# One mixer and MLP block kernel on a single core: the small pieces beside the big products are placed two at a time

## The reference

```python
proj = einsum('bsd,de->bse', rms_norm(x, norm_w), w_in)      # 6160 columns
# 4 GLA heads (dk 128, dv 256), 4 HGRN heads (dk 128, dv 128), each the recurrence
#   S_t = diag(g_t) S_{t-1} + k_t v_t^T,  o_t = S_t^T q_t
# 4 cross heads: softmax(q mk^T / sqrt(128)) mv over the memory's 256 tokens
mixed = concatenate([gla_o, hgrn_o, xo]) * silu(gate)        # each head rms-normed
x = x + mixed @ w_out
```

## Time and profile before

| | |
|---|---|
| median of 3 runs | 2051.71 us |
| time of the profiled execution | 2051.9 us |
| its span | 2050.1 us |
| PE busy | 2011.2 us, 98% of the span |
| PEld busy | 1687.5 us, 82% |
| DVE busy | 1070.6 us, 52% |
| ACT busy | 815.6 us, 40% |
| POOL busy | 762.3 us, 37% |
| chain that ended last | PE 81%, POOL 6%, DVE 6%, issue 3%, ACT 3% |

### The profile page before, as it was taken

How to read it: one execution, slowest core, us unless ns; L and a number is a source line. 1 busy time by engine, 2 the same in 40 slices (tenths; PEclk the granted TensorE clock), 3 DMA queues, 4 the chain that set the end, 5 groups by cost and what they waited for, 6 DMA issues and landing times.

```text
span 2050.1 us, 26312 instructions
## 1 busy us (share of the span) xinstructions
PE 2011.2 (98%) x10210; PEld 1687.5 (82%) x10210; DVE 1070.6 (52%) x1903; ACT 815.6 (40%) x1365; POOL 762.3 (37%) x441
## 2 busy tenths in 40 slices
PE   9999999999999999999999989999999999999997
PEld 7888988988988888888888867788888888888886
DVE  6264455446555365554589978897541211112125
ACT  5424232343434523132365575763544333222311
POOL 3421211111121334353359948695444443222220
PEclk9999999999999999999999999999999999999998
DMA  4311111011111586775355423232223232111112
GB/s 175 101 34 52 42 32 52 32 59 35 42 52 61 185 318 239 260 262 162 116 185 185 178 90 103 83 94 93 93 91 103 93 98 88 43 50 51 52 42 82
DMA packets 69564, 215.63 MB, mean 105 GB/s; under 512 B 7856, under 2 KB 8240, under 8 KB 69312
## 3 DMA queue, kind: packets, MB, share of 16 engines
q1 hardware_dynamic: 55472, 188.26, 27.4%
q10 hardware_dynamic: 13968, 25.70, 3.6%
HBM read 184.56 MB, written 29.36 MB: 104 GB/s over the span
## 4 chain that ended last, share of the span: by engine, by line
PE 81%; POOL 6%; DVE 6%; issue 3%; ACT 3%; DMA 0%; POOLq 0%; DVEq 0%; SPq 0%; ACTq 0%
PE B L1491 37%; PE B L1670 24%; PE B L1554 7%; POOL CO L2786 5%; PE B L1592 4%; DVE B L2214 1%; PE B L1619 1%; PE B L1616 1%; PE B L1622 1%; POOL WL L2742 1%; DVE HB L2214 1%; PE B L1655 1%; PE B L1639 1%; PE B L1579 1%; PE B L1539 1%
## 5 line engine op out<-in xcount | busy, mean ns | idle before, releaser
L1491 PE MATMUL B<-HB,WH 128*128 128x512 f32 x2976 | 933.2, 401 | 7.2 <-DVE UP L2214 3.6
L2742 POOL TENSOR_TENSOR WL<-RAW,WH 128x1024 fp32r<-128x1024 f32 x205 | 495.1, 2419 | 933.1 <-ACT WH L1886 932.0
L1491 PEld LDWEIGHTS B<-HB,WH 128*128 128x128 f32 x2976 | 549.0, 189 | 127.0 <-issue 17.6
L1491 PE MATMUL B<-HB,WL 128*128 128x512 f32 x1488 | 563.9, 392 | 1.4 <-POOL WL L2742 1.4
L1886 ACT ACTIVATE WH<-RAW 128x1024 fp32r<-128x1024 f32 x205 | 215.6, 1056 | 444.8 <-DMA RAW<-wall 425.9
L1491 PEld LDWEIGHTS B<-HB,WL 128*128 128x128 f32 x1488 | 280.7, 189 | 62.9 <-POOL WL L2742 2.9
L2214 DVE SCALAR_TENSOR_TENSOR RES<-B,modv,RES 128x512 f32<-128x512 f32 x144 | 105.3, 749 | 203.5 <-PE B L1670 176.5
L2214 DVE SCALAR_TENSOR_TENSOR B<-UP,vec,B 128x512 f32<-128x512 f32 x308 | 208.1, 751 | 0.0
L1670 PE MATMUL B<-HIDH,WH 128*128 128x512 f32 x512 | 185.5, 395 | 0.0
L1670 PE MATMUL B<-HIDH,WL 128*128 128x512 f32 x512 | 182.4, 389 | 0.0
L1670 PE MATMUL B<-HIDL,WH 128*128 128x512 f32 x512 | 182.4, 389 | 0.0
(11 more groups left out here) (246 smaller groups left out, 2532.2 us busy)
## 6 DMA issues: line engine op xcount, KB each, us to landing
RAW<-wall SPq DMA_DIRECT2D x204, 512.0 KB, 3.6
MODRAW<-wmod ACTq DMA_DIRECT2D x96, 256.0 KB, 5.0
WH<-parts SPq DMA_DIRECT2D x32, 512.0 KB, 3.3
WL<-parts SPq DMA_DIRECT2D x32, 512.0 KB, 4.2
RES<-xT SPq DMA_DIRECT2D x16, 512.0 KB, 7.6
oscr<-OT SPq DMA_DIRECT2D x32, 256.0 KB, 2.1
OI<-oscr SPq DMA_DIRECT2D x16, 512.0 KB, 5.3
parts<-WH SPq DMA_DIRECT2D x16, 512.0 KB, 5.3
```

The source lines that it names most:

```text
L1491: i = pe.matmul(bank, a[:, ks], hb(part, k, h), start=k == 0 and n == 0, stop=k == 7 and n == 2)
L2742: po.tensor_tensor(lo, raw, hi.bitcast(F32), ALU.subtract).then_inc(sig[f"w_lo{q % NW}"], 1)
```

## The change

`tick` gets a threshold `group[0]`. It is 2.0 from the first recurrent head to the last product of the mixers, and 1.0 elsewhere, where `tick` works as before. With 2.0 nothing is placed until one of the two lanes has a credit of 2.0. Then there are two rounds, and in each the recurrent lane places a step if its credit is at least 0.3, and so does the cross lane. Rates and costs of the steps are the same, and so are all instructions; only their order changes. Up to the gates' products 336 small pieces stood in 270 unbroken runs between big matmuls; now they stand in 156, of which 92 have two pieces, 29 one, 23 three, 7 four, 4 five and 1 six.

```diff
 PASS = 0.2133
+GROUP = 2.0
 ...
-    credit, rate, turn = [0.0, 0.0], [0.5, 0.0], [0]
+    credit, rate, turn, group = [0.0, 0.0], [0.5, 0.0], [0], [1.0]

     def tick(us):
         while due and now["pe"] >= due[0][0]:
             next_due()
         u_splits(at_unit[0] - 1)
         credit[0] += rate[0] * us
-        while credit[0] >= 1.0 and (bg or bg2):
-            credit[0] -= step()
+        credit[1] = credit[1] + rate[1] * us if bg3 else 0.0
+        if max(credit) >= group[0]:
+            least = 1.0 if group[0] == 1.0 else 0.3
+            for _ in range(2 if group[0] > 1.0 else 100):
+                if credit[0] >= least and (bg or bg2):
+                    credit[0] -= step()
+                if credit[1] >= least and bg3:
+                    credit[1] -= step_in(bg3)
         if not (bg or bg2):
             credit[0] = min(credit[0], 1.0)
-        credit[1] = credit[1] + rate[1] * us if bg3 else 0.0
-        while credit[1] >= 1.0 and bg3:
-            credit[1] -= step_in(bg3)
 ...
     rate[0] = RATE[0]
+    group[0] = GROUP
     for h in range(4):
 ...
     rate[0] = RATE[3]
+    group[0] = 1.0
     for h in range(2):
         gate_product(0, h)
```

## The result

The changed kernel takes 2066.29 us (median of 4 runs, 2064.80 to 2067.83) against 2050.49 us (4 runs, 2046.66 to 2052.34): ratio 1.0078 [1.0061, 1.0096], so slower by 0.8%. The forecast was 2067 us, slower. The median of before is 2050.49 and not 2051.71 because a fourth run was added. The profiled execution of the changed kernel took 2067.63 us, with a span of 2065.8; that of before had 2051.9 and 2050.1. So 15.7 us are to be explained.

A forecast was written before the change was run, and what follows sets the result against it. TensorE's own instruction list was taken as the bound. GLA pairs 4.0, HGRN 6.6, less 2.0, ScalarE 1.6, longer runs 6.8, less 1.9 gave 15.1 us on 2051.9: 2067 us, 0.7% slower, range 2059 to 2074.

The forecast's parts named there:

- Entries cost nothing with 128 columns: At runs of small pieces in the mixers: halving the entries (270 runs to 156) gives 0, at most 1 us.
- 64 columns: At the 64-column level: a crossing costs 0.32 us, one of two goes in six of eight heads, 1.9 us gained.
- Pairs of chunks, regular price: In adjacent chunks, the second waits for banks 6 and 7: GLA loses 4.0 us, HGRN 6.6 us.
- ScalarE busy ahead: 1.6 us: At chunk pairs: a ScalarE operation of 0.3 to 1 us ahead in a third of 26 pairs adds 1.6 us.
- Longer runs: 6.8 us: In longer runs of small pieces, a fourth use of three `S` banks waits for the first: nine places, 6.8 us together.
- Pairs of levels without cross steps: 0: At two adjacent level halves without cross steps: they are independent, in different banks, and cost nothing.
- Existing stops: TensorE's stops in the mixers before the change, within 8.9 us idle; the sum has no term for their going.
- rival 2: In the mixers, the new order misses existing stops, 6 us of idle goes, pair waits under 2 us: 2046 us; chance 0.07.
- Rival 3, the clock: In the mixers, stops bring the clock down, seven more such stretches, 12 us on top: 2079 us; chance 0.18.
- What would show it: From 100 to 700 us TensorE's idle rises from 8.9 to some 20 us, with `OSB`, `ST`, `AB` wait rows; afterwards only later.
- the three HGRN pairs of before: HGRN chunk pairs already adjacent before the change; their waits were taken off the sum at 2.0 us.

## Why the prediction was right

The time (2066.3 against 2067) and the sign were right, and so was the kind of cause: TensorE waits for drained banks. Its idle time in the mixers is 19.6 us against the 20 forecast. Much of the closeness is luck: the mixers got 13.5 us longer, not 15.1, and the start's -1.4 and the end's +3.6 of the clock are no part of the argument. By its steps:

- **Entries cost nothing with 128 columns.** Right. Of the 201 single pieces before, the six with the largest excess hold 6.1 us, all at waits; the other 195 have 0.65 us together, 0.003 each. So 114 entries fewer gave well under 1 us, as forecast.
- **64 columns.** Right, 0.34 for 0.32 per crossing, and that the crossing is the shape's is shown by the 96-column kernel. Six heads gain 0.34 each, 2.0 us for 1.9. The 2.8 of the table has head 5 in it too, whose two crossings (0.69) now stand in a run of six pieces and are counted there.
- **Pairs of chunks, regular price.** Right. GLA 0.32 and 0.36 for my 0.30 and 0.40, and 0.01 for 0; HGRN 0.42 to 0.49 for my 0.55. In sum 9.4 us for 10.6, and the bank is shown as the cause by the kernel with three.
- **ScalarE busy ahead: 1.6 us.** This term was mis-sized, and it did not follow from its own words: 0.3 to 1 us in a third of 26 pairs is 2.6 to 8.7 us. Four stops hold 9.0 us above the regular prices: 3.67 at 519, 3.23 at 366, 2.03 at 590 and 1.34 at 433. Few places are hit by 1 to 3 us each. The bound of 1.5 us from the earlier trace rows was too low: operations queue in a row of three on ScalarE. Two of the four are not what the term meant: that at 366 hangs on the order of the levels and waits for `KT`, no bank, and that at 590, 1.6 of the 9.0, is VectorE stretched beside GpSimd.
- **Longer runs: 6.8 us.** 5.9 measured, and nine runs for my nine places; the kernel with one lane per group takes most of it away. Single ones go from 0.3 to 1.5 us.
- **Pairs of levels without cross steps: 0.** Wrong by 3.5 us. The two halves do not wait for each other's banks, as argued, but the second half needs its scaling, and that one was stretched by GpSimd.
- **Existing stops.** I kept them as they were. In fact some 6 us of single stops went (1.70 at 331, 1.08 at 604, 0.83 at 618, four of 0.5), besides the 3.7 that only moved into the pairs. That is rival 2's mechanism, at just the 6 us it named, but without its outcome, since the pair waits were far above its 2 us.
- **Rival 3, the clock.** It added nothing in the mixers: the lower clock costs 3.0 us there, less than before (4.4), though there are more stops. Its mechanism is there all the same. The two stretches at the lower level, 3.4 us each from 367.5 and 524.5 us, stand right behind the two longest stops, and with three output banks each stop of some 5 us brought one. The other stops, of 2.03 us and less, brought none.
- **What would show it.** Idle time, `ST` and `AB` rows came as written. The row of the `AB` product for `OSB` with a dozen occurrences did not: it has two, because the view leaves out waits of 0.2 us. They show in the distances between starts alone. From 700 us on not everything was the same: the 3.6 us at the lower clock came there.

Measured less forecast, the errors are +7.4 (the four long stops, of which 1.6 is GpSimd's), +3.5 (levels), +0.9 (the rest) and +0.7 (the three HGRN pairs of before lost 1.3, not 2.0) against -9.8 (existing stops), -1.4 (clock), -1.2 (regular prices), -0.9 (longer runs) and -0.9 (64 columns). The sum was right to 1.6 us, its terms were not: that is a forecast helped by cancelling. What stays open is what makes the clock fall more often behind the mixers, and how to tell ahead which stops a new order lengthens and which it removes.

## What to carry to other kernels

- Before small pieces are put side by side, read for each the time from its last matmul to the end of its drain, and count the banks: a pair is free only if the matmuls between two uses of a bank last longer than that. Saving entries was worth something here only where the stationary operand went from 128 to 64 columns.
- On an engine that does both drains and long transformations, the price of a late drain is not its mean load but the queue in front of it at that moment; forecast it as few large stops. A new order moves all such stops, those that exist too, so neither keep nor drop them in the sum.
- A bank's worth is how long its longest holder holds it, not how long it takes to fill.

## What the runs showed of the hardware

- A stationary operand of 64 columns between ones of 128 costs 0.34 us for going in and out; 112 and 96 columns cost 0.00 to 0.03.
- These float32 passes are paced by the stationary side: with 64 moving columns the starts are 0.112, 0.098, 0.085 and 0.058 us apart for 128, 112, 96 and 64 stationary columns, and with 128 moving columns still 0.111.
- A pass that starts behind a wait takes longer to the next start: 0.21 us in place of 0.11 with 128 moving columns, 0.32 in place of 0.22 with 256, and 0.16 in place of 0.11 for a level's pass with 64 moving columns. It is the same behind a wait of 0.16 us and one of 2.57.
- One VectorE operation on two operands in SBUF takes 2.58 us instead of 0.42 beside GpSimd's subtraction of 128x1024, and 0.42 again without it. One on 128x4 takes 2.17 us beside it and 0.16 without.
